# Dilated attention: probabilities instead of values held stationary in the value product

## The reference, cut to what matters

```python
def dilated_prompt(q, k, v):
    ...
    for w, d in DIL_PATTERNS:
        ...
        o, lse = band_attn(sub(q), sub(k), sub(v), w // d)
    ...
    return combine_branches(outs, lses)

def combine_branches(outs, lses):
    wts = jax.nn.softmax(jnp.stack(lses), axis=0)
    y = sum(wts[i][..., None] * outs[i] for i in range(len(outs)))
```

## Time and profile before

| what | value |
|---|---|
| median of 3 runs | 2790.06 us (2787.67 to 2792.68) |
| profiled execution, its own time | 2794.43 us |
| profiled execution, span of the trace | 2792.4 us |
| mean granted TensorE clock | 0.999 of 2.4 GHz |
| TensorE matmul, busy | 2764.5 us (99%) |
| TensorE weight load, busy | 2656.7 us (95%) |
| VectorE, busy | 1728.8 us (62%) |
| ScalarE, busy | 897.8 us (32%) |
| GpSimd, busy | 1447.2 us (52%) |
| the four pairs' main stretches | about 1477 to 1694 us from the span's start |

### The profile page before, as it was taken

One profiled execution on the slowest core, in us unless ns is written; L12 is line 12 of the kernel. 1 busy time (PEld: TensorE's weight loads), 2 busy tenths in 40 slices (PEclk: granted clock), 3 DMA queues, 4 the chain that ended last, 5 costly groups with the idle time before them and its releaser, 6 DMA issues. The chain is left out here.

```text
span 2792.4 us, 61236 instructions
## 1 busy us (share of the span) xinstructions
PE 2764.5 (99%) x22943; PEld 2656.7 (95%) x22943; DVE 1728.8 (62%) x3178; ACT 897.8 (32%) x2009; POOL 1447.2 (52%) x1178
## 2 busy tenths in 40 slices
PE   9999999999999999999999999999999999999998
PEld 8888999999999999999998879999999999999998
DVE  5555743247866766887963346432477667668877
ACT  4333422232422222443413344222324222224433
POOL 2222343433577777777532112434335777777775
PEclk9999999999999999999999999999999999999999
DMA  4111124331232322633123331243312323226332
GB/s 140 38 30 31 60 97 152 123 119 38 77 121 75 121 106 106 213 122 129 55 89 116 106 122 47 94 156 121 121 39 77 121 75 121 106 106 210 125 130 77
DMA packets 85189, 286.95 MB, mean 103 GB/s; under 512 B 11230, under 2 KB 21470, under 8 KB 76056
## 3 DMA queue, kind: packets, MB, share of 16 engines
q10 hardware_dynamic: 46973, 152.08, 15.6%
q1 hardware_dynamic: 38051, 132.55, 14.4%
HBM read 225.26 MB, written 59.59 MB: 102 GB/s over the span
## 5 line engine op out<-in xcount | busy, mean ns | idle before, releaser
L682 POOL TENSOR_SCALAR w_hi<-w_raw 128x512 fp32r<-128x512 f32 x236 | 154.2, 671 | 952.8 <-PE linear L831 750.4
L686 POOL TENSOR_TENSOR w_lo<-w_raw,w_hi 128x512 fp32r<-128x512 f32 x420 | 587.5, 1410 | 104.3 <-ACT w_hi L1663 88.2
L831 PE MATMUL linear<-h_hi,w_hi 128*128 128x344 f32 x1134 | 372.8, 329 | 2.1 <-issue 1.4
L831 PE MATMUL linear<-h_lo,w_hi 128*128 128x344 f32 x1134 | 362.2, 319 | 0.0
L831 PE MATMUL linear<-h_hi,w_lo 128*128 128x344 f32 x1134 | 362.2, 319 | 0.0
L686 POOL TENSOR_TENSOR w_lo<-w_sum,w_hi 128x512 fp32r<-128x512 f32 x186 | 270.0, 1452 | 148.6 <-ACT w_hi L1663 147.8
L1219 PE MATMUL ps_scores<-c,w_hi 128*128 128x258 f32 x1512 | 288.5, 283 | 0.0
L1219 PE MATMUL linear<-c,w_hi 128*128 128x258 f32 x1344 | 247.3, 284 | 1.4 <-POOL w_lo L686 1.4
L831 PE MATMUL linear<-g_hi,w_hi 128*128 128x344 f32 x744 | 240.3, 323 | 0.0
L831 PE MATMUL linear<-g_hi,w_lo 128*128 128x344 f32 x744 | 237.7, 319 | 0.0
L831 PE MATMUL linear<-g_lo,w_hi 128*128 128x344 f32 x744 | 237.5, 319 | 0.0
(11 more groups left out here) (483 smaller groups left out, 7213.0 us busy)
## 6 DMA issues: line engine op xcount, KB each, us to landing
w_raw<-in_w SPq DMA_DIRECT2D x214, 512.0 KB, 3.7
hid_spill<-hid_out ACTq DMA_DIRECT2D x22, 1032.0 KB, 4.4
t_spill<-hid_joined ACTq DMA_DIRECT2D x20, 1032.0 KB, 3.9
y_val<-t_spill ACTq DMA_DIRECT2D x40, 516.0 KB, 4.0
kv_slotc<-in_mem_cache_k ACTq DMA_DIRECT2D x8, 2048.0 KB, 8.3
kv_slotc<-in_mem_cache_v ACTq DMA_DIRECT2D x8, 2048.0 KB, 10.4
w_more<-in_w SPq DMA_DIRECT2D x32, 512.0 KB, 5.5
y_val<-hid_spill ACTq DMA_DIRECT2D x30, 516.0 KB, 5.0
```

What stands on the lines that cost most here:

```text
L682: pool.tensor_scalar(out, src, 1.0, 0.0, ALU.mult, ALU.add).then_inc(sem["hi_split"], 1)
L686: return pool.tensor_tensor(out, src, hi.bitcast(F32), ALU.subtract).then_inc(sem[event], 1)
L831: mm = pe.matmul(out, w[:, slot, cols], a, start=(k == 0 and j == 0), stop=(k == n - 1 and j == 2))
```

## The change

The turned probabilities become the stationary operand, 32 columns (one class of queries) at a time, each on its own column group of 32; the values of a head, 64 columns, move. The result in `ps_o[:, 0:128]` is then queries x features. VectorE multiplies it by the reciprocal of each row's denominator for each head, into `drawn1` (`weigh`, for `scale`); TensorE transposes that (`right`), and ScalarE copies the result into its chunk of `mix1`, undoing the sorting (`lay`, for `fan`). `right(k-1)` and `lay(k-1)` stand behind T(k) in their queues. The semaphores `spread`, `fanned`, `laid` and `scaled` give way to `weighed`, `righted` and `placed`.

```diff
@@ pe, turn @@
                         pe.transpose(ps_t[0:BATCH_S, 384:512], sel["dil"][:], ident[:]).then_inc(sem["turned"], 1)
+                        right(QB - 1)
                         return
...
                         mm.then_inc(sem["turned"], 1)
+                    if k:
+                        right(k - 1)
+
+                def right(k):
+
+                    pe.wait_ge(sem["weighed"], at("weighed", ph, 0, k + 1))
+                    pe.wait_ge(sem["placed"], at("placed", ph, 0, k))
+                    c = P * (k % 2)
+                    pe.transpose(ps_o[:, P:2 * P], drawn1[:, c:c + P], ident[:]).then_inc(sem["righted"], 1)
@@ pe, mix @@
-                    pe.wait_ge(sem["scaled"], at("scaled", ph, 0, k))
+                    pe.wait_ge(sem["placed"], at("placed", ph, 0, k))
                     pe.wait_ge(sem["turned_in"], at("turned_in", ph, 0, done + 1))
                     for m in blocks_of(k, 0):
                         for h in range(2):
-                            r, at_ = HEAD * h, place_in_half(h, 0, m)
-                            mm = pe.matmul(ps_o[r:r + HEAD, 0:P], vnat1[:, kb + m, r:r + HEAD], pt1[:, at_:at_ + P],
-                                           start=(m == 0), stop=(m == nb - 1 and not far), skip_group_check=True)
+                            for c in range(CLASSES):
+                                at_ = place_in_half(h, 0, m) + FAR * c
+                                mm = pe.matmul(ps_o[FAR * c:FAR * c + FAR, HEAD * h:HEAD * h + HEAD], pt1[:, at_:at_ + FAR],
+                                               vnat1[:, kb + m, HEAD * h:HEAD * h + HEAD], start=(m == 0 and h == 0),
+                                               stop=(m == nb - 1 and not far), skip_group_check=True)
...
                         for b in blocks_of(k, 1):
-                            for c in range(CLASSES):
-                                for h in range(2):
-                                    r, at_ = HEAD * h, place_in_half(h, 1, b) + FAR * c
-                                    mm = pe.matmul(ps_o[r:r + HEAD, FAR * c:FAR * c + FAR], vfar1[:, b, P * c + r:P * c + r + HEAD],
-                                                   pt1[:, at_:at_ + FAR], start=False, stop=(b == blocks_of(k, 1)[-1]),
-                                                   skip_group_check=True)
+                            for h in range(2):
+                                for c in range(CLASSES):
+                                    at_, from_ = place_in_half(h, 1, b) + FAR * c, P * c + HEAD * h
+                                    mm = pe.matmul(ps_o[FAR * c:FAR * c + FAR, HEAD * h:HEAD * h + HEAD], pt1[:, at_:at_ + FAR],
+                                                   vfar1[:, b, from_:from_ + HEAD], start=False,
+                                                   stop=(b == blocks_of(k, 1)[-1]), skip_group_check=True)
                         mm.then_inc(sem["mixed"], 1)
-                    pe.wait_ge(sem["fanned"], at("fanned", ph, 0, k + 1))
-                    c = P * (k % 2)
-                    pe.transpose(ps_o[:, P:2 * P], drawn1[:, c:c + P], ident[:]).then_inc(sem["spread"], 1)
@@ act @@
-                def fan(k):
-
-                    act.wait_ge(sem["inverted"], at("inverted", ph, 0, BIAS_ORDER.index(k) + 1))
-                    if k >= 2:
-                        act.wait_ge(sem["spread"], at("spread", ph, 0, k - 1))
-                    c = 2 * (k % 2)
-                    copy(drawn1[:, P * (k % 2):P * (k % 2) + P].rearrange("p (h n) -> p h n", h=2),
-                         inv1[:, c:c + 2].rearrange("p (h n) -> p h n", n=1).to_broadcast([P, 2, HEAD])).then_inc(sem["fanned"], 1)
+                def lay(k):
+
+                    act.wait_ge(sem["righted"], at("righted", ph, 0, k + 1))
+                    qb = PIECES[k][0]
+                    copy(mix1[:, 4 + i, P * qb:P * qb + P].rearrange("p (a r) -> p r a", r=CLASSES),
+                         ps_o[:, P:2 * P].rearrange("p (r a) -> p r a", r=CLASSES)).then_inc(sem["placed"], 1)
...
                         if k == 6:
                             exponential(SCORE_ORDER[-1])
-                        fan(k)
+                        if k:
+                            lay(k - 1)
@@ dve @@
-                def scale(k):
...
-                    dve.tensor_copy(out, by_class(ps_o[:, P:2 * P])).then_inc(sem["laid"], 1)
-                    dve.wait_ge(sem["laid"], at("laid", ph, 0, k + 1))
-                    dve.tensor_tensor(out, by_class(ps_o[:, 0:P]), out, ALU.mult).then_inc(sem["scaled"], 1)
+                def weigh(k):
+
+                    dve.wait_ge(sem["mixed"], at("mixed", ph, 0, halves_until(k) + HALVES[k]))
+                    if k >= 2:
+                        dve.wait_ge(sem["righted"], at("righted", ph, 0, k - 1))
+                    by_head = lambda ap: ap.rearrange("p (h n) -> p h n", h=2)
+                    c = 2 * (k % 2)
+                    dve.wait_ge(sem["inverted"], at("inverted", ph, 0, BIAS_ORDER.index(k) + 1))
+                    dve.tensor_tensor(by_head(drawn1[:, P * (k % 2):P * (k % 2) + P]), by_head(ps_o[:, 0:P]),
+                                      inv1[:, c:c + 2].rearrange("p (h n) -> p h n", n=1).to_broadcast([P, 2, HEAD]), ALU.mult
+                                      ).then_inc(sem["weighed"], 1)
```

More of the change, by code:

```diff
@@ L214, in phases @@
                              "biased": len(BIAS_ORDER), "exped": n + 1, "inverted": QB + 1, "normed": 1,
-                             "turned": sum(HALVES), "turned_in": sum(HALVES), "mixed": sum(HALVES), "spread": QB, "fanned": QB, "laid": QB, "scaled": QB, "drawn": 1,
+                             "turned": sum(HALVES), "turned_in": sum(HALVES), "mixed": sum(HALVES), "weighed": QB, "righted": QB, "placed": QB, "drawn": 1,
                              "redrawn": 1, "mixed_out": 1}))
@@ L1532, in mix @@
                         pe.wait_ge(sem["turned_in"], at("turned_in", ph, 0, done + 1))
-                        pe.wait_ge(sem["scaled"], at("scaled", ph, 0, QB))
+                        pe.wait_ge(sem["placed"], at("placed", ph, 0, QB))
                         pe.wait_ge(loads["v_slot"], 16 * (5 + i))
@@ L2409, in step @@
                             copy(pt1[0:BATCH_S, 384:512], ps_t[0:BATCH_S, 384:512]).then_inc(sem["turned_in"], 1)
+                            lay(QB - 1)
                             return
@@ L3467, in step @@
                     elif what == "V" and k != "sample":
-                        scale(k)
+                        weigh(k)
                     if (what, k) == ("S", 6):
```

## The result

The changed kernel takes 2799.89 us in the median of 8 runs, before takes 2790.62 in 8 runs of the same chips; the ratio is 1.0033, 95% interval 1.0024 to 1.0043: slower by 9.3 us, where +11.4 was forecast (2801.5, range 2796 to 2812). The profiled execution has a span of 2799.7; it is one of the two slowest of its eight (2801.68).

A forecast was written before the change was run, and what follows sets the result against it. TensorE, holding matmuls for 99% of the span, was taken to bound the kernel. Three pairs' 8.6 us plus the last pair's 2.8 gave +11.4 on 2790.1: 2801.5 us, slower by 0.41%, range 2796 to 2812.

The forecast's parts named there:

- The wait: TensorE's transposition behind T(k) waits for VectorE's weigh, queued behind peaks; with savings, +2.86 us a pair, 8.6 for three.
- its sign: TensorE's idle time ahead of the 32 transpositions, released by weigh: together 15 to 20 us.
- The five stalled steps: Steps 0, 1, 3, 4, 5 of a pair, TensorE waiting for weigh: +1.13, +0.76, +0.39, +1.17, +0.30 us.
- hand-off: From weigh's end to TensorE's first following matmul: 0.20 us, low end 0.16, high end 0.38.
- Steps 2, 6, 7: Steps of a pair where far products save and little or no wait is left: -0.10, -0.50, -0.29 us.
- the moved transposition: Transposition moved from between products and transposes to behind the transposes: net -0.04 us a step, if it doesn't wait.
- The products: TensorE's value products: 0.22 us a block; near costs the same, far saves 0.23 a block, 1.8 a pair.
- Rival B: Same wait, but matmul records can't start closer than 0.026 us: +20.4, so 2810.5 us; chance 0.12.
- The far saving: Far products on TensorE: 0.23 us less a key block, eight blocks a pair.
- The last pair: Last head pair: early steps +2.1, then -0.27, -0.16, +0.55, and steps 5 to 7 +0.6; sum +2.8 us.
- Rival C: Waits half as long, low-end weigh and hand-off, full far savings even under waits: +6 us; chance 0.12.
- D: VectorE weighs before the peaks are through, so the transposition isn't delayed: -10 us, 2780; chance 0.06.

The follow-up runs named there:

- e5: Changed kernel with VectorE weighing twice in every step, first into a scrap tile: 2805.27 us, ratio 1.0058 to the kernel before.
- e2: Changed kernel with V ahead of S in each group of the first three pairs, on all engines: 2788.39 us, ratio 1.0002 to the kernel before.
- e9: Changed kernel with V first in three pairs, last pair's transposition and laying behind the next scoring, and weighing ahead of the splits: 2783.77 us, ratio 0.9979 to before.
- e1: Changed kernel without TensorE's transposition of the weighed result; ScalarE lays the rows unturned: 2779.25 us, ratio 0.9966 to the kernel before.
- e6: Changed kernel with ScalarE's lay(5) moved ahead of the last exponential: 2796.46 us, ratio 1.0027 to the kernel before.
- e4: Changed kernel with V ahead of S in three pairs, and the last pair's transposition and laying behind the next scoring: 2784.94 us, ratio 0.9985 to before.
- e3: Changed kernel with the last pair's transposition and laying behind the next scoring, lay(5) ahead of the last exponentials: 2794.89 us, ratio 1.0020 to the kernel before.
- e10_before_order: Kernel before the change, with V ahead of S in its first three pairs, as control for the order: 2792.19 us, ratio 1.0008.
- e8_busy: Changed kernel with 20 constant transpositions filling each of TensorE's two long waits in the last pair: 2799.96 us, ratio 1.0039 to the kernel before.

## Why the prediction was right, point by point

**The wait.** Shown. The idle time stands where it was put, ahead of the transposition and released by `weigh`, largest in steps 0 and 4, none in step 6; e5 lengthens it and the time by the operation's cost, e2 and e9 take it away, and the time with it. Its sum, 11.2, is under the 15 to 20 that I named as its sign, and in the first three pairs steps 0 and 4 have 0.79 and 1.00, where 1.1 was named. Measured as the start of the projection behind a step, from one step to the next (for step 0 from the step 7 of the pair before), the terms are:

| step | 0 | 1 | 2 | 3 | 4 | 5 | 6 | 7 | sum |
|---|---|---|---|---|---|---|---|---|---|
| predicted | +1.13 | +0.76 | -0.10 | +0.39 | +1.17 | +0.30 | -0.50 | -0.29 | +2.86 |
| measured | +1.00 | +0.64 | -0.31 | +0.28 | +1.02 | +0.20 | -0.33 | -0.36 | +2.14 |

The five stalled steps are each 0.10 to 0.15 too high. From the start of `weigh` to the start of the projection I took 0.39 + 0.20 = 0.59; measured is 0.43 in all five (1478.23 to 1478.66 in step 0): 0.29 for `weigh` and 0.14 for the hand-off. So both terms are at or under the low ends that I gave, and VectorE reaches `weigh` 0.01 to 0.06 later than I took it to. The row that I copied for `weigh` writes with a stride into its chunk and also reads and multiplies there; `weigh` writes contiguously. Which of these makes the 0.1 no run parts.

**Steps 2, 6, 7.** Step 2 was priced with a wait of 0.17 that didn't come, for the same two terms. Step 6 gained less: V(6) waits a little for `lay(5)` (the products start 0.39 behind the last projection's start instead of 0.25), and a series of transposes that follows products directly, and not another full-array transposition, is 0.05 to 0.06 longer (0.66 for four instead of 0.60). That also used up the 0.04 a step that I gave the moved transposition.

**The products.** As priced: near 20.8 against 20.2 busy, a block at 0.22 (32 near records in 0.63, so (0.63 - 0.22) / 31 = 0.013 a record). Far 16 in 0.41, (0.41 - 0.22) / 15 = 0.013 too, half of before. Rival B is out by this, and by e1. The far saving of 0.23 a block holds where no wait covers it: e2's groups with one far block are 0.21 to 0.26 shorter than before's.
The floor of 25 ns between starts in the Trainium skill (TensorE: Matmul & The Clock Gate, "Wait — 56ns, not 53.3ns?") does not hold here: records start 13 ns apart on average over four column groups. It may hold within one group, which gets a record only every 0.055: (0.63 - 0.41) / 4, from the 32 near and 16 far records of step 2.

**The last pair.** Predicted +2.8, measured +4.6. Its mechanism is as written: the chain VectorE, scoring, VectorE in steps 0 and 1, and V(6) behind the last exponential, which e6 confirms. What was not in the sum is the granted clock. The same code with the clock up all along (e2_v_first's last pair) takes 38.69, +2.77 over before, and its terms are near mine one by one: steps 0 and 1 +2.16 (predicted +2.1), step 2 -0.23 (-0.27), step 3 -0.22 (-0.16), step 4 +0.52 (+0.55), steps 5 to 7 +0.54 (+0.6). The difference of 1.85 lies from V(0) to V(1) (4.83 against 4.28) and from V(6) to V(7) (4.60 against 3.30), the two places with the clock at 1.2 GHz.

**Sum.** 0.72 too much in each of three pairs (2.2), 1.8 too little in the last: +11.0 in the trace for +11.4 forecast. That it came so near is in part luck: two errors of opposite sign, and one of them, the clock, is a thing that I had not thought of and that comes in some executions only. Rival C is half in the trace: `weigh` and the hand-off do cost their low ends, as it said, which is most of the 0.72. Its other half, far products that save even where the wait covers them, is not there. D asked for no wait and is out.

**Open.** When the low clock comes. In the profiled executions it came with both long waits of the changed kernel, with that of step 0 in e5 and e6, and behind waits of 1.1 and 0.5 in e4. It did not come with two waits of the same length in e2, with that of step 6 in e5 (2.27), with the same 1.1 and 0.5 in e3, or with 1.5 in e9 and in the kernel before. What it costs in the median isn't shown either.

## What to carry to other kernels

A helper operation that is cheap and on a half-idle engine costs what stands ahead of it in that engine's queue, once the full engine waits for it; read its start from the trace, not its length. Before moving such a wait, look for the order in which the helper's work comes first: here exchanging two steps in a table turned +9 us into 0, and with the last pair mended into -6. A new order needs its own control and its own reading of the waits: the same exchange cost the kernel before 0.9 us a pair, and in the changed one it brought a wait behind another engine. Exchanging the stationary and the moving operand cost nothing in these products (0.22 a near block with 128 columns moving on two column groups, and with 64 on four); other shapes weren't measured.

## What the runs showed of the hardware

- Four column groups of 32 with the full 128 rows take a record every 0.013 us with 64 columns moving; twice as close as the two groups of 64 with 32 columns moving (0.026 to 0.029), although these moved half as much. So the far products before were not bound by the columns that move: 32 columns took more than a quarter of what 128 took on the same two groups (0.026 a record against 0.056).
- ScalarE's copy of 128x128 within SBUF takes 0.31 written contiguously and 0.43 written at a stride of 4 elements (e1_unturned); out of PSUM to the same stride it takes 0.40. VectorE's two operations out of PSUM with that stride take 0.39 each, the multiplication with contiguous writes 0.29; their operands differ too.
- A transposition between products and scoring, both on column groups, costs 0.15 to 0.16 more than one in front of the transposes (e10_before_order, each of six groups).
- The granted clock fell to 1.2 GHz towards the end of TensorE's waits of 2.04 and 2.36 us in one execution, and did not at waits of the same length in another kernel's; 32 near records then take 1.08 instead of 0.63 to 0.65. With the waits filled by transpositions (e8_busy), its mean over the execution was 0.999 in five executions of five.
